# Fewer and later split matmuls, rotary tables in the feed-forward stage and spread sums in a three-pass fp32 transformer kernel

## The reference

```python
def first_block(...):
    x = x + hybrid_mixer(...)      # h @ w_in; 8 heads of gated delta rule, 8 heads of attention; @ w_out
    x = x + cross_attention(...)   # 4 heads over 256 memory tokens
    x = x + conv_ffn(...)          # (silu(causal_dwconv(h @ w_gate) + b) * (h @ w_up)) @ w_down, 5632 wide
    return rmsnorm(x, final_norm_g)

def second_block(x, positions, ...):
    cos, sin = _rope_tables(positions)          # 8 frequencies, the first 16 of 64 features turn
    for layer in range(2):
        if layer == 0:
            h = _mamba2_mixer(x, ...)           # @ a_w_in (10304 wide), 8 groups of ssm, @ a_w_out
        else:
            k_sh, v_sh = _shared_kv(x, kv_w, kv_b, cos, sin)
            h = _swa_mixer(x, k_sh, v_sh, cos, sin, b_w_in, b_q_bias, b_sinks, b_w_out)
        x = _layernorm(ALPHA * x + h, ln_g[layer], ln_b[layer])
    return x
```

## Time and profile before

| what | value |
|---|---|
| median of 3 runs | 2456.08 us (2455.59 to 2456.27) |
| the profiled execution's own time | 2455.53 us |
| its span in the trace | 2453.5 us |
| TensorE busy | 2408.2 us, 98% |
| VectorE busy | 1770.1 us, 72% |
| ScalarE busy | 1211.1 us, 49% |
| GpSimd busy | 505.7 us, 21% |
| read from HBM | 412.31 MB, 170 GB/s |

### The profile page before, as it was taken

One profiled execution on the slowest core, in us unless ns is written; L12 is line 12 of the kernel. 1 busy time (PEld: TensorE's weight loads), 2 busy tenths in 40 slices (PEclk: granted clock), 3 DMA queues, 4 the chain that ended last, 5 costly groups with the idle time before them and its releaser, 6 DMA issues. The chain is left out here.

```text
span 2453.5 us, 51551 instructions
## 1 busy us (share of the span) xinstructions
PE 2408.2 (98%) x20814; PEld 2367.7 (97%) x20814; DVE 1770.1 (72%) x2825; ACT 1211.1 (49%) x1918; POOL 505.7 (21%) x575
## 2 busy tenths in 40 slices
PE   7999999999999999999999999999999999999998
PEld 6999999999899999999999999999999999889998
DVE  6677646685666665655656888777887887888887
ACT  5433344554544444444444545544544554556554
POOL 1233310160200000000002312341221222521102
PEclk9999999999999999999999999999999999999999
DMA  6433335565555556556556645545554445444453
GB/s 216 157 126 123 123 125 178 186 205 168 163 189 192 197 177 209 195 179 211 191 179 190 195 161 170 172 165 171 171 178 158 163 151 183 151 154 157 157 166 117
DMA packets 124503, 418.29 MB, mean 170 GB/s; under 512 B 13796, under 2 KB 17644, under 8 KB 124012
## 3 DMA queue, kind: packets, MB, share of 16 engines
q1 hardware_dynamic: 124268, 415.00, 51.5%
HBM read 412.31 MB, written 3.68 MB: 170 GB/s over the span
## 5 line engine op out<-in xcount | busy, mean ns | idle before, releaser
L784 PE MATMUL b<-XH,WH 128*128 128x256 f32 x4213 | 1187.5, 282 | 21.9 <-DVE WL L1661 17.7
L785 PE MATMUL b<-XL,WH 128*128 128x256 f32 x4224 | 1173.9, 278 | 0.0
L786 PE MATMUL b<-XH,WL 128*128 128x256 f32 x4224 | 1173.3, 278 | 0.0
L1244 ACT ACTIVATE WH<-WR 128x1024 fp32r<-128x1024 f32 (+2 forms) x811 | 814.4, 1011 | 466.3 <-PE b L786 458.7
L1661 DVE TENSOR_TENSOR WL<-WR,WH 128x1024 fp32r<-128x1024 f32 (+2 forms) x811 | 993.3, 1235 | 14.5 <-ACT WH L1244 14.2
L784 PEld LDWEIGHTS b<-XH,WH 128*128 128x128 f32 x4213 | 793.4, 188 | 33.2 <-issue 17.0
L785 PEld LDWEIGHTS b<-XL,WH 128*128 128x128 f32 x4224 | 798.0, 189 | 0.6
L786 PEld LDWEIGHTS b<-XH,WL 128*128 128x128 f32 x4224 | 794.9, 188 | 0.0
L784 PE MATMUL b<-OH,WH 128*128 128x256 f32 x1675 | 468.4, 280 | 7.1 <-DVE WL L1661 5.7
L785 PE MATMUL b<-OL,WH 128*128 128x256 f32 x1680 | 466.5, 278 | 0.0
L786 PE MATMUL b<-OH,WL 128*128 128x256 f32 x1680 | 466.2, 278 | 0.0
(11 more groups left out here) (410 smaller groups left out, 2323.3 us busy)
## 6 DMA issues: line engine op xcount, KB each, us to landing
WR<-a_w_in SPq DMA_DIRECT2D x160, 512.0 KB, 3.7
WR<-w_in SPq DMA_DIRECT2D x112, 512.0 KB, 3.6
WR<-w_gate SPq DMA_DIRECT2D x88, 512.0 KB, 4.0
WR<-w_up SPq DMA_DIRECT2D x88, 512.0 KB, 4.1
WR<-a_w_out SPq DMA_DIRECT2D x64, 512.0 KB, 3.4
WR<-b_w_in SPq DMA_DIRECT2D x64, 512.0 KB, 3.7
WR<-w_down SPq DMA_DIRECT2D x64, 384.0 KB, 3.5
WR<-w_down SPq DMA_DIRECT2D x64, 320.0 KB, 2.9
```

The lines of the kernel that those rows point to most:

```text
L784: mm(ps, WH[:, slot, at:at + P], xh, start=(k == 0), stop=False)
L785: mm(ps, WH[:, slot, at:at + P], xl, start=False, stop=False)
L786: m = mm(ps, WL[:, slot, at:at + P], xh, start=False, stop=(k == p["kt"] - 1))
L1244: act.activation(WH[:, s, 0:n], WR[:, r, 0:n], ACT.Copy).then_inc(*act_w.up(i))
```

## The change

Six things change. (1) The table `OPENED` goes; `opened(steps)` computes the places from the list of steps. Between two small steps with matmuls it counts tiles; if a run has 24 tiles or more (11 or more when the small step ahead is one of "ns", "sums" or a norm), the fifth tile of the run is split. One more place, `("fg", 6)` at tile 4, is always split. (2) `rot` begins where the feed-forward stage begins, 8 slots in and with a step every 4 slots, has its steps "s0" and "s1" for ScalarE's sine apart from "c0" and "c1", and works in constants that are no longer used there (`lev`, `onehot`), in place of T1 and T2. (3) ("mid", 1) starts 24 slots later, not 1, and takes a step every 4 slots. (4) In "stat" GpSimd makes the power before its two additions; in layer 0 the additions move into the steps "pair" 1 and 2. (5) `centred(8)` moves from "pair" 2 to the end of "stat". (6) In layer 1 the pair 14 is centred by TensorE.

```diff
@@ ln of the plan
         self.step("ln", layer, "sub", 6)
+        if layer:
+            self.step("ln", layer, "sub", 14)
@@
-OPENED = {
-    (("gk", 0, 1), 4), (("gz", 1, 1), 12), (("gz", 2, 1), 12), (("gz", 3, 1), 12), (("xkv", 2), 8), (("fg", 0), 14),
-    (("fu", 0), 2), (("sc", 0), 8), (("x3", 0), 8), (("z1", 1), 4), (("z1", 4), 4), (("z1", 7), 4), (("so", 0, 14), 4),
-    (("so", 1, 14), 4), (("so", 2, 14), 4), (("bo", 0, 9), 4),
-}
+def small(step):
+    kind, name = step[0], step[-1]
+    if kind in ("dt", "ln"):
+        return True
+    return kind in SMALL and (name in SMALL[kind] or kind == "gdn" and name[0] in "ab")
+
+def opened(steps):
+    places, here, run, last = set(), None, 0, None
+    for step in [*steps, ("dt",)]:
+        if small(step):
+            sure = last is not None and (last[-1] in ("ns", "sums") or last[0] == "norm")
+            if here is not None and run >= (11 if sure else 24):
+                places.add(here)
+            here, run, last = None, 0, step
+        elif step[0] == "half":
+            key, k0, k1 = step[1], step[3], step[4]
+            if run <= 4 < run + k1 - k0:
+                here = (key, k0 + 4 - run)
+            if key == ("fg", 6) and k0 == 4:
+                places.add((key, k0))
+            run += k1 - k0
+    return places
@@ make_plan
     q.norm(2)
     q.late = False
+    q.begin(("rot",), ["a", "n0", "r0", "c0", "s0", "n1", "r1", "c1", "s1"], 4, 8)
...
-    q.begin(("rot",), ["a", "n0", "r0", "c0", "n1", "r1", "c1"])
     for part in (2, 3):
...
-    q.begin(("mid", 1), [("x", m) for m in range(16)] + [None] * 12 + ["s"], 1, 1)
+    q.begin(("mid", 1), [("x", m) for m in range(16)] + [None] * 3 + ["s"], 4, 24)
@@ half_of
-                if (key, k) in OPENED:
+                if (key, k) in plan.opened:
@@ rot, ScalarE
-            if name[0] == "c":
+            if name[0] == "s":
                 which = int(name[1])
                 w.wait_ge(*dve_rot.of("c", which))
-                act.activation(T2(0)[:, half(which)], T1(6), ACT.Sin).then_inc(*act_rot.up(which))
+                act.activation(turned[:, half(which)], turned[:, half(which)], ACT.Sin).then_inc(*act_rot.up(which))
@@ ln, VectorE
                 centred(2)
+                centred(8)
...
-                    if 2 * j in (4, 6):
+                    if 2 * j in ((4, 6, 14) if layer else (4, 6)):
...
-                if j in (2, 5):
-                    centred(8 if j == 2 else 14)
+                if j == 5 and layer == 0:
+                    centred(14)
@@ ln, GpSimd
+                w.wait_ge(*dve_ln.of("ms", layer))
+                power(SM(21), SM(20)[:, 2:4], 2).then_inc(*pool_ln.up("r", layer))
                 w.wait_ge(*dve_ln.of("mu", layer))
-                for m in (10, 12):
-                    pair = XT[:, m:m + 2, :]
-                    w.wait_ge(*act_ln.of("sq", layer, 15))
-                    pool.tensor_tensor(pair, pair, rep(T1(7), 2), add).then_inc(*pool_ln.up("sub", layer, m))
-                    if m == 10:
-                        w.wait_ge(*dve_ln.of("ms", layer))
-                        power(SM(21), SM(20)[:, 2:4], 2).then_inc(*pool_ln.up("r", layer))
+                w.wait_ge(*act_ln.of("sq", layer, 15))
+                if layer:
+                    centred(layer, 10)
+                    centred(layer, 12)
             elif layer == 0 and name == "pair":
...
+                if j in (1, 2):
+                    centred(0, 8 + 2 * j)
```

More of the change, by code:

```diff
@@ L369 @@
 MPLACE = list(range(16, 22)) + list(range(8)) + [8, 9]
+SMALL = {
+    "gdn": ("sums", "eg", "rows", "tv", "kk", "tt", "l0", "v0", "st", "xx", "v1", "o", "ns", "nr"), "att": ("lg", "v", "bk", "pv", "ns", "nr"),
+    "xat": ("lg", "tr", "o"), "ssm": ("cb", "x0", "x1", "ds", "st", "ec", "l0", "l1", "yo", "y0", "y1", "ns", "nr"),
+    "swa": ("lg", "bk", "pv"), "norm": ("sums", "rows"), "mem": ("tok", "rows"), "time": ("t",), "mid": ("s",), "toep": ("t",),
+    "ba": ("p", "b"), "kvt": ("t",), "vd": ("t",),
+}
+def small(step):
[19 more added lines that the diff above has]
+    return places
 def make_plan():
@@ L494, in make_plan @@
     q.steps = [s for s in q.steps if s[0] not in ("issue", "split") or s[1] < n + (s[0] == "split")]
+    q.opened = opened(q.steps)
     return q
@@ L604, in program @@
     ident, U, L, ones = cc("ident"), cc("U"), cc("L"), cc("ones")
+    turned = cc("lev", 0, 2 * S)
     spent = POFF["gdn_cw"][0]
@@ L2209, in rot @@
         def rot(name):
-            an, nn, rr = T1(4), T1(5), T1(6)
-            niv = T2(1)[:, 0:S].bitcast(I32)
+            an, nn = cc("lev", 2 * S, S), cc("onehot", 0, S)
+            niv = nn.bitcast(I32)
             two_pi = 2 * math.pi
@@ L2217, in rot @@
             which = int(name[1]) if len(name) > 1 else 0
+            rr = turned[:, half(which)]
             if name == "a":
-                w.wait_ge(*pe_ssm.of("nr", 6))
-                w.wait_ge(*act_os.of("ssm", 27))
-                w.wait_ge(*pe_dt.of("t"))
+                w.wait_ge(*pool_gdn.of("ao", 3, 6))
+                w.wait_ge(*pe_toep.of("t"))
                 w.wait_ge(*ld_pos.of("pos"))
@@ L2242, in rot @@
                 dve.scalar_tensor_tensor(rr, nn, -c3, rr, ALU.mult, ALU.add).then_inc(*dve_rot.up("r3", which))
-            else:
+            elif name[0] == "c":
                 w.wait_ge(*dve_rot.of("r3", which))
@@ L2258, in ln_squares @@
             if m == 1:
-                w.wait_ge(*(pe_swa.of("lg", 15, 1) if layer else act_rot.of(1)))
+                w.wait_ge(*(pe_swa.of("lg", 15, 1) if layer else pe_dt.of("t")))
             else:
@@ L2317, in ln @@
                     dve.scalar_tensor_tensor(XT[:, m, :], x, pc("ln_g", 16 * layer + m), rstd, ALU.mult, ALU.mult).then_inc(
-                        *dve_ln.up("b", layer, m, frees=frees if m in (3, 5, 7) else None))
-                if j in (2, 5):
-                    centred(8 if j == 2 else 14)
+                        *dve_ln.up("b", layer, m, frees=frees if m in ((3, 5, 7, 15) if layer else (3, 5, 7)) else None))
+                if j == 5 and layer == 0:
+                    centred(14)
                 if layer == 0:
@@ L2330, in rope @@
                 for i, o in ((a, a + 32), (a + 32, a)):
-                    last = dve.tensor_tensor(T1(9)[o:o + 32, :], source[i:i + 32, :], T2(0)[i:i + 32, 0:S], ALU.mult)
+                    last = dve.tensor_tensor(T1(9)[o:o + 32, :], source[i:i + 32, :], turned[i:i + 32, 0:S], ALU.mult)
                     last.then_inc(*dve_swa.up("u", o, *who))
@@ L2614, in ln, with centred @@
         def ln(layer, name, j=None):
+            def centred(layer, m):
+                pair = XT[:, m:m + 2, :]
+                pool.tensor_tensor(pair, pair, rep(T1(7), 2), add).then_inc(*pool_ln.up("sub", layer, m))
             if name == "stat":
@@ L2636, in rope @@
                 w.wait_ge(*dve_swa.of("u", 64, *who))
-            pool.tensor_tensor(to, to if source is None else source, T2(0)[:, S:2 * S], mult).then_inc(*pool_swa.up("cos", *who))
+            pool.tensor_tensor(to, to if source is None else source, turned[:, S:2 * S], mult).then_inc(*pool_swa.up("cos", *who))
             w.wait_ge(*pool_swa.of("cos", *who))
```

## The result

| | before | after |
|---|---|---|
| median, same chip (5 runs each) | 2455.67 us (2455.17 to 2456.27) | 2439.36 us (2438.67 to 2442.0) |
| ratio after / before, 95% interval | | 0.9936 [0.9922, 0.9951] |
| profiled execution, own time / span | 2455.53 / 2453.5 us | 2442.0 / 2439.8 us |

The kernel became 16.3 us faster. The forecast was 2445.1 us, 5.7 us too slow and inside its range.

A forecast was written before the change was run, and what follows sets the result against it. The prediction took matmul pace, TensorE's waits and two normalization tails to bound the kernel; -3.9 - 2.1 + 0.3 - 4.6 - 0.7 = -11.0 us, from 2456.08 to 2445.1 us, whole range 2438.5 to 2454.

The forecast's parts named there:

- What bounds the kernel: Whole kernel: TensorE busy 98%, so only matmul pace (113.3 or 117.8 ns), TensorE's waits and two normalization tails move the end.
- Splits, -3.9: 56 new split places, 16 old ones gone: 22 slow stretches turn quick, -9.2 + 6.7 - 1.8 = -4.3 us, taken as -3.9.
- Tables, -2.1: Rotary tables leave the stretch of `so` part 2: 2.5 us go, 0.4 already counted with the splits, so -2.1 us.
- Loads in the feed-forward stage, +0.3: Feed-forward stage: each sine with its table loads takes ScalarE 3.0 us, just covered by the weights' 3.3 us lead; +0.3 us.
- GpSimd's sums, -4.6: First attention tiles: spreading the additions removes TensorE's 3.1 us wait and 1.6 us of half clock; -4.6 us.
- Normalizations, -0.7: Last normalization: VectorE's chain loses two operations, ScalarE becomes the bound, -0.7 us; first normalization taken as 0.
- That splits turn nothing: Rival on the slow stretches: splits leave the rhythm unchanged and cost 4.9 us instead of gaining 3.9; 2453.9 us, chance 0.13.
- Stalls by the sines: Rival in the feed-forward stage: the sines' table loads make TensorE wait 2 to 3 us each; +5, 2450 us, chance 0.09.
- by the additions: Rival in the attention tiles: spread additions meet each rotation, TensorE waits 0.5 us in eight tiles; +4, 2449 us, chance 0.10.
- The slow feed-forward stage: Rival: the split at `("fg", 6)` leaves 5,750 matmuls slow, 25.6 us lost; 2470.7 us, chance 0.08.

The follow-up runs named there:

- e2_tables: The kernel before with only the rotary tables moved to the feed-forward stage, sine in its own steps: 2452.25 us against 2455.08.
- e4_norms: The kernel before with only the edits of the two normalizations: 2454.22 us against 2455.08.
- e3_sums: The kernel before with only GpSimd's sums started 24 halves later and spread to one each four halves: 2448.94 us against 2455.08.
- e5_nosplit: The changed kernel with no split tile: 2469.7 us over 12 runs, three at 2441.3 to 2445.2 and nine at 2468.9 to 2471.4.
- e8_sine_in_c: The changed kernel with ScalarE's sine right behind VectorE's range reduction, without steps "s0" and "s1": 2440.38 us.
- e10_list26: The changed kernel with a chosen list of 26 split places, two of them in the feed-forward stage: 2436.07 us against 2456.08 for the kernel before.
- e12_ninth: The changed kernel with a second split at the ninth tile of the 55 runs split at the fifth: 2445.54 us.
- e7_head: The changed kernel with each split at the first tile of its stretch, not the fifth: 2443.68 us.
- e6_slowonly: The changed kernel with 24 chosen split places, none in the feed-forward stage: 2463.65 us against 2455.82 for the kernel before.

## Why the prediction was right, step by step

The mechanisms were right and the time lay inside the range, 5.7 us from its middle. About half of that is in the terms below, and the other half in how executions of one kernel differ.

- **What bounds the kernel: right.** Pace, waits and tails. The pace is what counted most, both in the gain and in what could have been lost.
- **Splits, -3.9: right in size.** 1,969 slow matmuls fewer x 4.45 ns is 8.8 us, 40 more splits x 0.11 us is 4.4, so -4.4; alone they measured -4.3. All 55 splits outside the half clock ended quick; only the one at 16.95 us, at the end of the start, where matmuls are 0.21 us apart, stayed slow. That a split in the running flow ends quick "whatever rhythm it was in" was argued from the nearest rows only, and is what the 156 cases above showed. The head places that lost theirs (`bo` chunk 9, two of `gz`) now run slow, as allowed for. One reading of my rows was luck of the trace: the split at `("x3", 0)`, which left 293 matmuls slow in before, is in the same place in e2_tables and e4_norms and left them quick, 1.3 us less.
- **Tables, -2.1: too small.** This is the term that was mis-sized. The stretch with the tables holds 423 matmuls and the one that I compared it with 436: the latter is four tiles longer, 12 x 0.113 = 1.4 us. For equal work it is 51.7 against 47.8. Between the starts of the same tiles the trace of after has 4.0 us less than before, of which the splits are 0.4. So -3.6 in place of -2.1. The counts were in my own rows, and I compared only the lengths.
- **Loads in the feed-forward stage, +0.3: nothing.** TensorE waits for neither. The lead of the weights in the `fg` and `fu` where the sines run, never under 3.3 us in before (in `dn` it is 1.3, which I had overlooked), is down to 0.95 us at its smallest in after. With the sine in the step "c" it is down to 0.15, and TensorE loses 0.14 us. The step of its own is worth those 0.8 us of lead; in the whole time it can't be measured.
- **GpSimd's sums, -4.6: right.** Both segments of the attention tiles together are 5.0 us shorter, 0.3 of it by the splits (the first `wq` turned quick, less the price of two); in e3_sums 4.5. The rotation no longer waits behind an addition, and no half clock follows.
- **Normalizations, -0.7: half right.** The end gave the 0.7, in this trace. With the same edit it gives 0.6 to 1.1 in four traces and 1.9 in six (e4_norms, e5_nosplit, e8_sine_in_c, e10_list26 to e12_ninth), and the granted clock tells them apart. At the same place, while TensorE centres, in after and then in e10_list26:
```profile
2426.90:2430.30 3.40, 3.40 (x11) 2.66 (x11) 1.67 (x6) 0.00 (x0) 2.86 (x3) 0.50 0.00 0
2422.30:2425.70 3.40, 3.22 (x18) 2.56 (x17) 2.85 (x8) 1.10 (x3) 2.93 (x3) 1.00 0.00 0
```
My -0.7 was worked out from a trace with the half clock in it; without it the same code ends 1.3 us sooner. The first one cost 0.6 where I took 0, inside its bounds of -0.7 and +1.5. The meeting is priced above: 0.87 became 2.40 us. By the rule of the Trainium skill (SBUF — State Buffer, Who interferes with whom) that was to be expected, and this trace agrees again: 1.53 us longer beside an addition of 1.47.
- **What is left.** Terms as measured in the trace: -4.4 - 3.6 + 0 - 4.7 + 0.6 - 0.7 = -12.8, where the profiled execution has -13.7. The other 0.9 are in no term: up to `fg` 0 and in groups 0 to 7 after is 0.5 us shorter each than its slow matmuls and splits make it. The median is another 2.6 us lower. What differs between executions is the half clock, in the last normalization (1.3 us, above) and in the first: the interruption ahead of `bkv` lasted 9.55 us in the traces of before and after and 8.34 in that of e10_list26, 1.2 us. TensorE there, first in after and then in e10_list26:
```profile
2086.49 1.06 PE L1217 MATMUL b<-XT,con 128*128 128x256 f32 x2
2087.34 1.06 PE L1218 MATMUL b<-t1s,con 128*128 128x256 f32 x2
```
```profile
2082.49 0.59 PE L1219 MATMUL b<-XT,con 128*128 128x256 f32 x2
2082.92 0.59 PE L1220 MATMUL b<-t1s,con 128*128 128x256 f32 x2
```
The code of this step is the same. I had written that TensorE works on these at half clock "right up to the rows" and took that for given; it is so in some executions only. The two together are 2.5 us, near the 2.6, and the mean granted clock of after's executions points the same way: 0.998 in the two slowest and 0.999 or 1.000 in the three fastest. These have no trace, so it isn't shown.
- **The rivals.** That splits turn nothing: out. Stalls by the sines and by the additions: out, no such wait, though 0.95 us was all that was left for the sines. The slow feed-forward stage: it didn't come, but the mechanism is real and its size right (27.8 us against 25.6 for a smaller part of the stage). I had its cause the wrong way round: I feared that the split at `("fg", 6)` would turn the stage slow, and it is the stage without splits that is slow, in nine executions of twelve by their times; in e8_sine_in_c that very split turned it quick. The two splits there protect some 28 us for 0.2 us: the 34 executions of after and of the six variants of it that have two or more splits in that stage (e7_head to e12_ninth) took at most 2447.4 us, where the nine took 2468.9 or more.

## What to carry to other kernels

Look at the distance between matmuls, not at how busy TensorE is: two rhythms 4% apart can sit at the same clock, last for hundreds of microseconds and differ between executions of one kernel. A break of the rhythm that costs 0.11 us, put four tiles into a running stretch, with no wait right ahead of it, pays for itself from 25 slow matmuls on: take it in the short stretches that come out slow in every trace, and in the very long ones as an insurance, quick or not in the trace at hand. A stall of 0.14 us, which no view of waits lists, can start a slow stretch; one did, in e8_sine_in_c. And before two windows are compared by length, compare their counts.

## What the runs showed of the hardware that I had not expected

- The same restart, with the same instructions ahead of it, ended in either rhythm: of the twelve executions of e5_nosplit three took some 2443 us and nine 2470; the quick stage is traced there, the slow one in e6_slowonly.
- A split with ten or more matmuls of flow ahead ended quick in 383 cases of 383, 156 of them out of the slow rhythm, while nine of 56 at the head of a stretch left it slow. Right behind a wait it is uncertain too: 13 slow matmuls in one trace and 379 in another, at the same place. Why there are two rhythms stays open.
- Whether the granted clock fell to half in the interruption ahead of `bkv`, and in the last normalization, was not the same for the same code: two pairs of 128x256 matmuls took 1.06 us in after and 0.59 in e10_list26. What decides it stays open.
